# A two-layer decoder trunk on one core: the last 256 output columns by token tile, the closing LayerNorm on VectorE, attention scores over all 128 rows

## The reference

```
for l in range(2):
    h = x @ w_in[l]                       # 2048 -> retention, latent attention, mLSTM, memory, gate z
    y = concat(ret, mla, mls, memo) * silu(z)
    x = LayerNorm(alpha * x + y @ w_out[l]) * ln_g[l] + ln_b[l]
```

```
q = concat([q[..., :128], rope(q[..., 128:])])     # 64 rotary columns per head
k = concat([kv[..., :128], broadcast(rope(k_pe))])
scores = q @ k.T * (128 + 64) ** -0.5              # causal, then softmax
```

## Time and profile before

| | |
|---|---|
| median of 3 runs | 949.21 us (948.3 to 949.36) |
| the profiled execution | 948.5 us, of which the span from first to last instruction is 946.6 us |
| busy: PE, PE weight loads, DVE, ACT, POOL | 98%, 88%, 67%, 52%, 2% of the span |
| granted TensorE clock, mean | 0.992 |
| HBM traffic | 169.53 MB read, 2.11 MB written, 181 GB/s over the span |
| last matmul starts / last pass of VectorE ends | 927.3 / 942.5 us |

### The profile page before, as it was taken

One profiled execution on the slowest core, in us unless ns is written; L12 is line 12 of the kernel. 1 busy time (PEld: TensorE's weight loads), 2 busy tenths in 40 slices (PEclk: granted clock), 3 DMA queues, 4 the chain that ended last, 5 costly groups with the idle time before them and its releaser, 6 DMA issues.

```text
span 946.6 us, 15684 instructions
## 1 busy us (share of the span) xinstructions
PE 924.6 (98%) x5876; PEld 835.5 (88%) x5876; DVE 633.8 (67%) x1261; ACT 496.1 (52%) x928; POOL 23.2 (2%) x23
## 2 busy tenths in 40 slices
PE   8999999999999999999999999999999999999991
PEld 7899998888789999888998999888877999988891
DVE  5867677667654765665759577867566557767666
ACT  5654764534455454544676456654444544554451
POOL 0000000000000000000000000000000000000004
PEclk9999999999999999999999999999999999999996
DMA  8875446645444555564765755554354544556642
GB/s 341 305 272 166 146 149 200 221 157 175 129 146 155 177 160 185 190 178 136 244 183 185 262 214 172 176 179 153 111 172 140 158 155 157 180 183 215 234 145 90
DMA packets 52156, 172.67 MB, mean 182 GB/s; under 512 B 6248, under 2 KB 6384, under 8 KB 51440
## 3 DMA queue, kind: packets, MB, share of 16 engines
q1 hardware_dynamic: 52080, 171.66, 56.2%
HBM read 169.53 MB, written 2.11 MB: 181 GB/s over the span
## 4 chain that ended last, share of the span: by engine, by line
PE 97%; DVE 1%; DMA 1%; issue 0%; SPq 0%; DVEq 0%; ACT 0%
PE acc L1122 18%; PE acc L1126 17%; PE acc L1123 17%; PE acc L1132 11%; PE acc L1138 11%; PE acc L1134 11%; PE work L858 2%; PE work L1001 1%; DVE X L1577 1%; PE work L1037 1%; PE work L919 1%; PE work L961 1%; PE work L1036 1%; DMA raw<-in_w 1%; PE work L863 1%; PE work L865 1%
## 5 line engine op out<-in xcount | busy, mean ns | idle before, releaser
L1168 DVE TENSOR_TENSOR lo<-raw,hi 128x512 fp32r<-128x512 f32 (+2 forms) x640 | 400.9, 640 | 285.9 <-ACT hi L828 281.0
L828 ACT ACTIVATE hi<-raw 128x512 fp32r<-128x512 f32 (+2 forms) x640 | 372.4, 590 | 357.9 <-PE acc L1126 183.4
L1122 PE MATMUL acc<-hi,xh 128*128 128x512 f32 (+2 forms) x608 | 222.8, 372 | 0.0
L1123 PE MATMUL acc<-hi,xl 128*128 128x512 f32 (+2 forms) x608 | 215.4, 360 | 0.0
L1132 PE MATMUL acc<-xh,hi 128*128 128x256 f32 x768 | 194.1, 285 | 0.0
L1134 PE MATMUL acc<-xl,hi 128*128 128x256 f32 x768 | 192.5, 283 | 0.0
L1126 PE MATMUL acc<-lo,xh 128*128 128x512 f32 (+2 forms) x608 | 169.2, 360 | 0.0
L1134 PEld LDWEIGHTS acc<-xl,hi 128*128 128x128 f32 x768 | 146.8, 191 | 0.2
L1132 PEld LDWEIGHTS acc<-xh,hi 128*128 128x128 f32 x768 | 146.7, 191 | 0.2
L1122 PEld LDWEIGHTS acc<-hi,xh 128*128 128x128 f32 x608 | 114.5, 188 | 17.4 <-issue 2.7
L1123 PEld LDWEIGHTS acc<-hi,xl 128*128 128x128 f32 x608 | 114.7, 189 | 14.6
(11 more groups left out here) (258 smaller groups left out, 999.3 us busy)
## 6 DMA issues: line engine op xcount, KB each, us to landing
raw<-in_w SPq DMA_DIRECT2D x255, 512.0 KB, 3.7
raw<-in_w SPq DMA_DIRECT2D x50, 256.0 KB, 2.7
raw<-in_w SPq DMA_DIRECT2D x16, 328.0 KB, 3.0
Y<-in_wuq SPq DMA_DIRECT2D x2, 1152.0 KB, 7.7
Y<-in_x_t SPq DMA_DIRECT2D x4, 512.0 KB, 8.6
X<-in_x SPq DMA_DIRECT2D x4, 512.0 KB, 4.7
gb<-in_gb SPq DMA_DIRECT2D x1, 2048.0 KB, 7.4
Y<-in_gb SPq DMA_DIRECT2D x1, 2048.0 KB, 9.9
```

Of the source, the lines that this page charges most:

```text
L828: act.activation(hi[:, t % RING, 0:w], raw[:, s, (t % 2) * w:(t % 2 + 1) * w], ACT.Copy)\
L1122: pe.matmul(o, ah[:, kk, q], hi[:, s, 0:w], start=k == 0, stop=False)
L1123: pe.matmul(o, al[:, kk, q], hi[:, s, 0:w], start=False, stop=False)
L1168: dve.tensor_tensor(lo[:, t % RING, 0:w], raw[:, s, (t % 2) * w:(t % 2 + 1) * w], hi[:, t % RING, 0:w].bitcast(F32), ALU.subtract).then_in ...
```

## The change

Three things are edited.

1. **The last chunk of layer 1, slots 304 to 319.** ScalarE and VectorE write hi and lo of these tiles not into the ring but each into its own place in `ml` and `mh`, and no longer wait for TensorE there. TensorE does all 16 tiles for token tile 0 and then all 16 for token tile 1. `residual(3)` of layer 1 moves from slot 308 to behind all remainders. Token tile 0 gets its last residual, its statistics, its root and its closing passes first, and then token tile 1 the same.
2. **The closing passes.** All are on VectorE, which does for token tile 0 two gain and two bias passes of 1024 columns, for token tile 1 four and four of 512; ScalarE and GpSimd have no part beyond the root. Gain passes are followed by a wait for their own end (`link`). SP stores two blocks of 512 KB and four of 256 KB.
3. **The scores.** `krT` becomes twice as large: copy 0 has zeros in rows 64 to 127, copy 1 in rows 0 to 63. The rotary product runs over all 128 rows of `qrT` (two heads one above the other) against copy h % 2, so the other head's rows meet zeros. `kpeT` writes the two halves by one ScalarE instruction each. Two memsets ahead of all others on VectorE make the zeros once.

```diff
+    if _c < NOUT - 2:
+        _put(DVE_AT, (OUT0 + _c + 1) * KT + 4, "residual", _c)
+    else:
+        _put(FIRST_DVE, (OUT0 + _c + 1) * KT + 4, "residual", _c)
...
+        def place(l, t, ring):
+            if stays(l, t):
+                return (ml if ring is hi else mh)[:, t % KT, 0:CHUNKS[LAST][1]]
+            return ring[:, t % RING, 0:CHUNKS[t // KT][1]]
...
-                    act.activation(krT[:, :], bank(l, ("kpeT", 0))[:, 0:SEQ], ACT.Copy)
+                    for r in range(2):
+                        half_ = slice(r * ROT, (r + 1) * ROT)
+                        m = act.activation(krT[half_, r, :], bank(l, ("kpeT", 0))[half_, 0:SEQ], ACT.Copy)
...
-                        m = pe.matmul(o[:, c0:c1], qrT[r, h // 2, q], krT[r, 0:c1 - c0], start=False, stop=True)
+                        m = pe.matmul(o[:, c0:c1], qrT[:, h // 2, q], krT[:, h % 2, 0:c1 - c0], start=False, stop=True)
...
+            for i in range(NT):
+                for k in range(KT):
+                    if i == 0:
+                        pe.wait_ge(hi_done.sem, hi_done.at(l, t))
+                    pe.matmul(o, ah, place(l, t, hi), start=k == 0, stop=False)
+                    pe.matmul(o, al, place(l, t, hi), start=False, stop=False)
+                    if i == 0:
+                        pe.wait_ge(lo_done.sem, lo_done.at(l, t))
+                    m = pe.matmul(o, ah, place(l, t, lo), start=False, stop=k == KT - 1)
+                m.then_inc(first_rows.sem if i == 0 else tile_used.sem, 1 if i == 0 else KT)
...
         def _(dve):
+            dve.memset(krT[ROT:P, 0, :], 0.0)
+            dve.memset(krT[0:ROT, 1, :], 0.0).then_inc(kr_zero.sem, 1)
             dve.memset(half[:, :], -0.5)
...
+            link(residual(c - 1))
+            dve.wait_ge(gb_in.sem, 16)
+            for i in range(NT):
+                (wait for first_rows, or for the whole chunk)
+                link(dve.scalar_tensor_tensor(xc, xc, ALPHA, A(CHUNKS[LAST][0], i)[:, 0:D_MODEL - OUTCOL[c]], ...))
+                link(dve.bn_stats(ln_stats[:, i, c, :], xc))
+                stand_alone(dve)
+                link(dve.bn_aggr(ln_mv[:, i, :], ...))
+                dve.tensor_scalar(ln_stats[:, i, 0, 0:1], ln_mv[:, i, 1:2], LN_EPS, None, ALU.add).then_inc(ln_var.sem, 1)
+                w = FINAL_WIDTH[i]              # 1024, 512
+                ahead = 2 * 512 // w            # 1, 2
+                for n in range(0, D_MODEL + ahead * w, w):
+                    (gain pass of block n, linked; bias pass of the block `ahead` before it, then finished + 1)
```

More of the change, by code:

```diff
@@ L230 @@
 MEM_PIECES = [(0, 1), (1, 1), (2, 2), (4, 2), (6, 2)]
-POOL_BIAS, DVE_BIAS = [0, 1, 2, 3, 4], [5, 6, 7]
-STORE_ORDER = [0, 1, 2, 5, 3, 6, 7, 4]
+LAST = NCH - 1
+FINAL_WIDTH = [1024, 512]
+FINAL = [(i, n) for i in range(NT) for n in range(0, D_MODEL, FINAL_WIDTH[i])]
 def pair_at(m):
@@ L431, in stand_alone, with stays @@
             eng.sem_inc(alone.sem, 1)
+        def stays(l, t):
+            return l == DEPTH - 1 and t >= LAST * KT
+        def place(l, t, ring):
+            if stays(l, t):
+                return (ml if ring is hi else mh)[:, t % KT, 0:CHUNKS[LAST][1]]
+            return ring[:, t % RING, 0:CHUNKS[t // KT][1]]
         def bank_of(l, job):
@@ L570, in _ @@
                                      .rearrange("p o n -> p (o n)")).then_inc(gb_in.sem, 16)
[L571 to L579, removed]
+            for b, (i, n) in enumerate(FINAL):
+                sp.wait_ge(finished.sem, b + 1)
+                sp.dma_start(out[i * P:(i + 1) * P, n:n + FINAL_WIDTH[i]], X[:, i, n:n + FINAL_WIDTH[i]])\
+                  .then_inc(stored.sem, 16)
+            sp.wait_ge(stored.sem, len(FINAL) * 16)
         @block.gpsimd
@@ L597, in _ @@
                     root(rstd[:, 0:4], stats[:, 0:4, 0], 4).then_inc(ret_pow.sem, 1)
+                if l == DEPTH - 1:
+                    for i in range(NT):
+                        pool.wait_ge(ln_var.sem, ln_var.at(l, i))
+                        root(ln_rstd[:, i:i + 1], ln_stats[:, i, 0, 0:1], 1).then_inc(ln_pow.sem, 1)
+                    break
                 pool.wait_ge(ln_var.sem, ln_var.at(l, 0))
@@ L826, in _ @@
                         act.wait_ge(raw_full[s].sem, raw_full[s].at(l, t // 2 // RAW))
-                    act.wait_ge(tile_used.sem, tile_used.at(l, t - RING))
-                    act.activation(hi[:, t % RING, 0:w], raw[:, s, (t % 2) * w:(t % 2 + 1) * w], ACT.Copy)\
+                    if not stays(l, t):
+                        act.wait_ge(tile_used.sem, tile_used.at(l, t - RING))
+                    act.activation(place(l, t, hi), raw[:, s, (t % 2) * w:(t % 2 + 1) * w], ACT.Copy)\
                        .then_inc(hi_done.sem, 1)
@@ L1101, in _ @@
                          "ret_scores": ret_scores, "ret_out": ret_out, "retT": retT_}
-                for t in range(SLOTS):
+                for t in range(SLOTS if l < DEPTH - 1 else LAST * KT):
                     c, k = divmod(t, KT)
@@ L1569, in _ @@
                 dve.tensor_scalar(ln_nmu[:, :], ln_mv[:, :, 0], -1.0, None, ALU.mult).then_inc(ln_mean.sem, 1)
+            l, c = DEPTH - 1, NOUT - 1
+            link(residual(c - 1))
             dve.wait_ge(gb_in.sem, 16)
[L1573 to L1585, removed]
+            for i in range(NT):
+                if i == 0:
+                    dve.wait_ge(first_rows.sem, 1)
+                else:
+                    wait_chunk(dve, l, LAST)
+                xc = X[:, i, OUTCOL[c]:D_MODEL]
+                link(dve.scalar_tensor_tensor(xc, xc, ALPHA, A(CHUNKS[LAST][0], i)[:, 0:D_MODEL - OUTCOL[c]],
+                                              ALU.mult, ALU.add))
+                link(dve.bn_stats(ln_stats[:, i, c, :], xc))
+                stand_alone(dve)
+                link(dve.bn_aggr(ln_mv[:, i, :], ln_stats[:, i, :, :].rearrange("p c s -> p (c s)")))
+                dve.tensor_scalar(ln_stats[:, i, 0, 0:1], ln_mv[:, i, 1:2], LN_EPS, None, ALU.add).then_inc(ln_var.sem, 1)
+                w = FINAL_WIDTH[i]
+                ahead = 2 * 512 // w
+                for n in range(0, D_MODEL + ahead * w, w):
+                    if n < D_MODEL:
+                        blk = X[:, i, n:n + w]
+                        link(dve.scalar_tensor_tensor(blk, blk, ln_mv[:, i, 0:1], gb[:, 0, n:n + w],
+                                                      ALU.subtract, ALU.mult))
+                    if n >= ahead * w:
+                        at = slice(n - ahead * w, n - ahead * w + w)
+                        blk = X[:, i, at]
+                        dve.wait_ge(ln_pow.sem, ln_pow.at(l, i))
+                        dve.scalar_tensor_tensor(blk, blk, ln_rstd[:, i:i + 1], gb[:, 1, at], ALU.mult, ALU.add)\
+                           .then_inc(finished.sem, 1)
```

38 lines of the change are left out of this document (16 added, 22 removed).

## The result

| | before | after |
|---|---|---|
| median | 948.75 us (4 runs, 947.98 to 949.36) | 935.78 us (4 runs, 935.64 to 936.26) |
| profiled execution / its span | 948.5 / 946.6 us | 935.7 / 933.9 us |
| granted TensorE clock, mean | 0.992 | 0.995 |

The ratio is 0.9866 (95% interval 0.9854 to 0.9877), 13.0 us less. Beside its variants the changed kernel was timed twice more: 936.43 against 948.38 (0.9877, 0.9862 to 0.9891) and 936.35 against 948.14 (0.9875, 0.9861 to 0.9890), 12.0 and 11.8 us less. The forecast was 937.3, 11.95 us less, with a range of 934.8 to 940.8. Of the 12.7 us between the two profiled spans, 0.5 lie ahead of the first head of `mla_scores`, 6.05 between there and the first matmul of the last chunk (916.12 before, 909.59 now), and 6.2 behind it.

What follows compares the result with a forecast made beforehand. TensorE was taken as the bound (97% of the chain), with VectorE and the stores behind its last matmul. Scores 6.4 plus tail 6.0 minus start 0.45 made 11.95 us less: 937.3 us from 949.2, range 934.8 to 940.8.

Steps and rivals of the forecast that it cites:

- The scores: `mla_scores`: row-count changes cost TensorE 0.79 us a head, over eight heads; all would go, gaining 6.4 us.
- The start: Two added memsets delay SP's first weight transfer: 0.45 us lost, range 0 to 0.55.
- The last chunk: TensorE waits about 1 us at token tile 0 behind late transfers; last remainder ends at 922.7 (922.15 to 923.4).
- Rival B: Last chunk: transfer burst much slower, last remainder at 925, gain 9.6 us, time 939.6; chance 0.12.
- The tail on VectorE: One row of VectorE instructions from last remainder at 922.7 to 937.7; with the stores, 6.0 us gained (4.8 to 7.1).
- Rival D: The scores' gain is real, but links and one engine's serial row eat the tail's gain: 943 us; chance 0.03.
- Slower passes (C): Tail: VectorE's 512-column passes stay near 1.7 us without GpSimd, 16 us more, 953 us; chance 0.03.
- The sum: Scores 6.4 plus tail 6.0 minus start 0.45: 11.95 us less, giving 937.3 us against the median.

Runs made afterwards that it cites:

- closing_dve: Kernel before with all eight closing scale-and-bias passes on VectorE, last chunk in the old order: 945.45 us against 948.39, ratio 0.9969.
- act_scales: Kernel before with GpSimd's five additions given to VectorE, ScalarE's five scaling passes kept, blocks stored in their own order: 945.21 us, one run.
- tail_only: Kernel before with only the new last-chunk order and closing passes on VectorE, scores as before: 942.05 us against 948.39, ratio 0.9933.
- slot 313: Changed kernel with `residual(3)` of layer 1 behind the remainder of that slot, not behind all remainders: 935.75 us beside the changed kernel's 936.43.
- slot 308: Changed kernel with `residual(3)` of layer 1 left at that slot, as before the change: 935.58 us beside the changed kernel's 936.35.
- after_again: The changed kernel once more, unaltered, beside its variants on the same chip: 936.43 us against 948.38 for the kernel before, ratio 0.9877.

## Why the prediction was right

- **The scores (6.4).** Right in place and in what triggers the loss, a little high in size: 0.75 us a head from the first to the eighth, 6.0 in all, where the sum had 0.79 and 6.4; 6.2 measured alone, 3.0 for half of the changes of row count. Whether it is a drain or a weight load that is no longer hidden stays open. It could be read before the run because another step of the same kernel, `ml_scores`, had the same products without the change of rows.
- **The start (0.45 lost).** Wrong. The step that failed is "the memset's end and SP's issue coincide, so I take 0.45". They coincided by chance: in the kernel before, the last of the seven increments comes at 1.38 and the memset happens to end at 1.42. With two more memsets in front, the last increment comes at 1.43, before the memset of `tmp` begins, and SP went out 0.05 later. The first of the weight pairs on the chain took 5.98 us instead of 6.47 to arrive in this profile, and TensorE was 0.48 ahead of the kernel before at the first head (233.51 against 233.99). That is the scatter of the start and not the change: in four other profiles this pair took 6.17 to 6.92 with the memsets first, and 6.04 to 6.49 in six without them in front (in the other two profiles the chain runs another way).
- **The last chunk.** TensorE's wait was forecast as 1 us, at token tile 0, behind the last transfers; it was 1.1, about half of it already at slot 314. The last five pairs went out at 908.0, 908.7, 909.4, 910.4 and 911.9, which is the forecast's order of times, moved by the 6.5 us of the start and the scores, within 0.3. The last remainder was forecast for 6.6 us after the chunk's first matmul (922.7 against 916.1); it came after 6.45 (916.05 against 909.6). In the two later profiles of the changed kernel it was 6.8 and 7.2, and TensorE lost 1.4 and 1.8 us. The range of that term, 6.0 to 7.3, holds all. Rival B, a last remainder at 8.9, did not come.
- **The tail on VectorE.** 15.0 us forecast from the last remainder to the last pass, 15.2 measured (916.05 to 931.23). Passes of 1024 columns took 1.3 with a link, as forecast. The stores' end was 2.7 instead of 2.8 behind. In all 6.3 us measured alone against 6.0. Rival D falls with that.
- **Slower passes (C)** fell by `closing_dve` and `act_scales`: without GpSimd they took 0.67 apart, with ScalarE beside them too. The prediction counted six slow passes in the kernel before; there were five (starts at 932.12, 933.80, 935.47, 937.15 and 938.81), as many as GpSimd's additions. Its sum does not use the count.
- **The sum.** 11.95 forecast; 13.0, 12.0 and 11.8 measured. The near hit is helped by two errors that cancel: the scores were some 0.4 too high by the traces and the start's 0.45 was not paid. The tail was 0.3 low. Of the 1.5 us between the forecast 937.3 and the first 935.8, 0.5 is the kernel before, which came out at 948.75 and not 949.2; the other 1.0 is gone in the later two groups.
- What the prediction did not see: `residual(3)` behind all remainders costs some 0.7 us against leaving it where it was. I had it as "where it delayed the remainders", and took the move as a plain part of the sum. VectorE's idle time in the last chunk would have covered it, up to the point where TensorE sets the end.

## What to carry to other kernels

Look for stretches where a busy engine takes more than its instructions do in a twin step elsewhere in the same trace: here four times 0.2 us per head stood in the chain and in no list of waits. Padding the product with zeros up to the full row count cost TensorE nothing here and took away the change of row count. Where padding is not possible, doing all products of one row count together took away half of it. At the end of this kernel, sharing the last passes with ScalarE and GpSimd was a loss of 2.9 us against VectorE alone. Splitting the last product by rows, so that the first rows are closed while the others are still multiplied, was a gain. Small steps that are still due belong into the waits of that stretch, not behind it.

## What was not expected of the hardware

- VectorE's increments of semaphores overtook its memsets: SP's transfer, which waits for the last of seven increments behind a 512-column memset of 0.48 us, went out 0.07 us before that memset had even begun.
- VectorE's gain passes and GpSimd's additions, both with two operands in SBUF, took 1.75 and 1.7 us side by side; without GpSimd the passes take 0.74. In the changed kernel it is GpSimd's root that is longer, 1.52 and 0.99 us against 0.69, beside passes that kept their time.
- A change of the row count cost about 0.2 us in each direction, also when the next matmul is of another type (0.43 instead of 0.23 us for the 512-column matmul of the stream), and there is none for the same rows with zeros in them.
- The first real matmuls were 0.21 us apart in some profiles and 0.12 in others of kernels that start with the same instructions (`tail_only` and the kernel before, slot 313 and slot 308), though the profile's granted clock says 1.00 for the first ten microseconds in both. How long it lasted differed between three profiles of the changed kernel itself: to 6.3, 7.0 and 10.0 us. The last of these is `after_again`. Its stretch from 9 to 10 us, and one of the kernel before from 8 to 9 us (us, TensorE busy with its instructions, granted clock, DMA share, GB/s), both with 256-column matmuls and TensorE busy throughout:

```profile
9.00:10.00 1.00, 1.00 (x7) 1.00 1.06 430
```

```profile
8.00:9.00 1.00, 1.00 (x11) 1.00 0.97 381
```

Seven matmuls and eleven, at the same 1.00: the distance of the matmuls has to be read, not the column. What decides it was not tried.
